# Attention probabilities transposed in 32x32 blocks on VectorE, with their partition groups exchanged by DMA through DRAM, in a hybrid encoder layer

## The reference, cut to what matters

```python
q_blocks = q_b.reshape(B, nb, Q_BLOCK, MLA_HEADS, hq).transpose(1, 0, 3, 2, 4)
scale = 1.0 / math.sqrt(hq)
def attend(qblk):
    s = jnp.einsum('bhqd,bhkd->bhqk', qblk, k_t).astype(jnp.float32) * scale
    p = jax.nn.softmax(s, axis=-1)
    return jnp.einsum('bhqk,bhkd->bhqd', p.astype(v_t.dtype), v_t)
```

## Time and profile before

| | |
|---|---|
| median of 3 runs | 1946.63 us |
| profiled execution | 1945.29 us, span from first to last instruction 1943.3 us |
| busy, share of the span | PE 97%, DVE 72%, ACT 54%, POOL 7% |
| MLA steps | first exponentials at 128.3 us, last at 523.3 us |
| first instruction of the GLA head (`gate_logits`) | 544.93 us |

### The profile page before, as it was taken

The page is one execution under the profiler, slowest core; times in us unless marked ns, Lnnn a source line. Parts: engine busy times, 40 slices in busy tenths (PEclk is TensorE's granted clock), DMA queues, the critical chain, the costliest instruction groups (busy, mean ns, idle before and its releaser), DMA issues.

```text
span 1943.3 us, 27074 instructions
## 1 busy us (share of the span) xinstructions
PE 1881.8 (97%) x9428; PEld 1598.5 (82%) x9428; DVE 1391.7 (72%) x1955; ACT 1049.3 (54%) x1726; POOL 135.8 (7%) x147
## 2 busy tenths in 40 slices
PE   9999999999999999999999999994799999999997
PEld 8988888888878888888888888884688888888886
DVE  4478777778865656657765348546799898998986
ACT  6476666555552434344434223321577777877775
POOL 1021101001000000000000000000000101001010
PEclk9999999999999999999999999997899999999999
DMA  6110000000321202022444463535899999999992
GB/s 208 44 43 7 23 23 18 23 25 18 125 62 32 66 23 77 11 76 87 139 156 150 140 205 109 184 130 197 318 379 400 391 401 399 392 400 390 400 391 77
DMA packets 147481, 327.57 MB, mean 169 GB/s; under 512 B 18080, under 2 KB 72736, under 8 KB 147232
## 3 DMA queue, kind: packets, MB, share of 16 engines
q1 hardware_dynamic: 142640, 309.59, 43.1%
q0 software_dynamic: 4752, 16.78, 3.4%
HBM read 287.92 MB, written 38.40 MB: 168 GB/s over the span
## 4 chain that ended last, share of the span: by engine, by line
PE 91%; DVE 5%; ACT 2%; DMA 1%; issue 1%; POOL 1%; SPq 0%; DVEq 0%; ACTq 0%; POOLq 0%
PE ps L1078 24%; PE ps L1080 24%; PE ps L1079 24%; PE ps L1067 7%; PE ps L1165 3%; PE ps L1373 1%; PE ps L1204 1%; PE ps L1203 1%; PE ps L1385 1%; PE ps L1357 1%; PE ps L1527 1%; PE ps L1383 1%; DVE top_i L2478 1%; DVE top_v L2477 1%; DMA xs<-in_x 1%
## 5 line engine op out<-in xcount | busy, mean ns | idle before, releaser
L1651 DVE TENSOR_TENSOR w_lo<-w_raw,w_hi 128x1024 fp32r<-128x1024 f32 x384 | 442.5, 1218 | 54.1 <-ACT w_hi L3054 53.9
L3054 ACT ACTIVATE w_hi<-w_raw 128x1024 fp32r<-128x1024 f32 x384 | 370.8, 1053 | 12.4 <-DMA w_raw<-in_w_gate_e 12.1
L1078 PE MATMUL ps<-w_hi,xeT_hi 128*128 128x512 f32 x512 | 201.0, 393 | 1.9 <-DVE xeT_lo L1651 1.0
L1080 PE MATMUL ps<-w_hi,xeT_lo 128*128 128x512 f32 x512 | 199.6, 390 | 0.0
L1079 PE MATMUL ps<-w_lo,xeT_hi 128*128 128x512 f32 x512 | 199.3, 389 | 0.0
L1651 DVE TENSOR_TENSOR d_lo<-d_raw,d_hi 128x1024 fp32r<-128x1024 f32 (+1 forms) x66 | 67.1, 1027 | 123.1 <-ACT d_hi L2716 118.5
L1078 PE MATMUL ps<-hT_parts,d_hi 128*128 128x512 f32 x368 | 144.7, 393 | 0.0
L1080 PE MATMUL ps<-hT_parts,d_lo 128*128 128x512 f32 x368 | 143.4, 390 | 0.0
L1079 PE MATMUL ps<-hT_parts,d_hi 128*128 128x512 f32 x368 | 143.3, 389 | 0.0
L985 POOL TENSOR_TENSOR stat<-stat,minus_half 128x4 f32<-128x4 f32 (+3 forms) x56 | 54.3, 971 | 1177.7 <-DVE stat L1648 1177.6
L1886 DVE TENSOR_REDUCE row_max<-ps 128x1 f32<-128x1024 f32 x64 | 78.3, 1224 | 79.1 <-PE ps L1204 79.1
(11 more groups left out here) (436 smaller groups left out, 4343.7 us busy)
## 6 DMA issues: line engine op xcount, KB each, us to landing
w_raw<-in_w_gate_e SPq DMA_DIRECT2D x128, 512.0 KB, 6.9
w_raw<-in_w_up_e SPq DMA_DIRECT2D x128, 512.0 KB, 6.9
w_raw<-in_w_down_e SPq DMA_DIRECT2D x128, 512.0 KB, 5.8
d_raw<-in_w_in SPq DMA_DIRECT2D x80, 256.0 KB, 3.3
gates_T<-stage SPq DMA_DIRECT2D x16, 512.0 KB, 2.6
sg<-gates_T SPq DMA_DIRECT2D x16, 512.0 KB, 3.6
stage<-mla_out_T SPq DMA_DIRECT2D x12, 512.0 KB, 5.3
xs<-in_x SPq DMA_DIRECT2D x8, 512.0 KB, 12.4
```

The source lines that it names most:

```text
L1078: pe.matmul(out_ap, a_hi, b_hi, start=start, stop=False)
L1080: return pe.matmul(out_ap, a_lo, b_hi, start=False, stop=stop)
L1651: return dve.tensor_tensor(dst, whole, high.bitcast(F32), ALU.subtract)
L3054: nc.scalar.activation(w_hi[:, n % RING, :], w_raw[:, n % RAW, :], ACT.Copy).then_inc(hi_ok, 1)
```

## The change

The transposition leaves PE. DVE transposes the normalised tile in 32x32 blocks (`squares_T`), within each group of 32 partitions. Blocks then still stand in the wrong group of partitions. SP writes each group of 32 partitions to DRAM (4 DMAs of 128 KB, `turn_probs`), waits for them, and reads the tile back as 128 rows of 4 KB, straight into `pT_lo`. ACT rounds it into `pT_hi` (one instruction from SBUF) and POOL subtracts in place to make `pT_lo`. `probs` has two buffers in place of three, `squares_T` has one. Columns of `pT_hi` and `pT_lo` are in another order, which a slice in `values` follows.

The order changes too: DVE normalises and transposes tile t at the end of step t, in place of normalising t-1 in the middle of it; the load of the hidden rows for the GLA stage is cut in 8 pieces of 512 KB, each waiting for the one before, among the turns of the last tiles; the second pair of `project_qk` comes before `values(7, 1)`.

```diff
+            def turn_probs(t):
+                sp.wait_ge(p_tr, t + 1)
+                if t:
+                    sp.wait_ge(p_in, 16 * t)
+                rows = p_dram[t % SLOTS].rearrange("(j b) q x -> b j q x", b=SQ)
+                for q in range(Q4):
+                    sp.dma_start(rows[:, :, q, :],
+                                 squares_T[q * SQ:(q + 1) * SQ].rearrange("b j c a -> b j (c a)")).then_inc(p_out, 16)
+                sp.wait_ge(p_out, 16 * Q4 * (t + 1))
+                group = t // Q4
+                if group >= 2:
+                    sp.wait_ge(pv_mm, group - 1)
+                sp.dma_start(probs_part(pT_lo, t).bitcast(F32),
+                             p_dram[t % SLOTS].rearrange("p q (c a) -> p q c a", a=SQ)).then_inc(p_in, 16)
...
-            for i in range(MH):
...
+            for i, n in STEPS:
+                if i < MH:
+                    turn_probs(8 * i + n)
...
+                if i >= MH - 1 and 2 <= 8 * i + n - 8 * (MH - 1) < 2 + KD:
+                    k = 8 * i + n - 8 * (MH - 1) - 2
...
+                    if k:
+                        sp.wait_ge(hT_in, 16 * k)
+                    sp.dma_start(hT_again[:, k, :], h_dram[k]).then_inc(hT_in, 16)
...
+            def probs_low(t):
+                pool.wait_ge(pt_hi, t + 1)
+                low = probs_part(pT_lo, t)
+                pool.tensor_tensor(low, low.bitcast(F32), probs_part(pT_hi, t).bitcast(F32),
+                                   ALU.subtract).then_inc(pt_lo, 1)
...
-            def probs_T(t):
-                pe.wait_ge(p_ok, t + 1)
-                for b in range(2):
...
-                    transpose4(4 + b, P, [probs[:, t % 3, (4 * b + j) * P:(4 * b + j + 1) * P]
-                                          for j in range(4)]).then_inc(p_tr, 1)
...
-                if tile_at(i, n) is not None:
-                    probs_T(tile_at(i, n))
+                if (i, n) == (MH, 2):
+                    for k in range(EARLY_ROWS, 4):
+                        project_qk(0, 0, k, first=True)
...
-                dve.tensor_scalar(probs[:, t % 3, :], probs[:, t % 3, :], row_inv[:, n:n + 1], None,
+                dve.tensor_scalar(probs[:, t % 2, :], probs[:, t % 2, :], row_inv[:, n:n + 1], None,
                                   ALU.mult).then_inc(p_ok, 1)
+                dve.wait_ge(p_ok, t + 1)
+                if t:
+                    dve.wait_ge(p_out, 16 * Q4 * t)
+                dve.transpose(squares_T[:], probs[:, t % 2, :].rearrange("p (c j b) -> p j c b", c=NT, j=Q4)) \
+                    .then_inc(p_tr, 1)
...
             def probs_high(t):
...
+                act.wait_ge(p_in, 16 * (t + 1))
+                nc.scalar.activation(probs_part(pT_hi, t), probs_part(pT_lo, t).bitcast(F32), ACT.Copy).then_inc(pt_hi, 1)
```

More of the change, by code:

```diff
@@ L993, in _, with keys_power, keys_rotary @@
                 rsqrt(stat[:, 1:3, t], mean_sq, mean_count(1, t), rstd)
-            for h in range(MH):
+            def keys_power(h):
                 rsqrt(stat[:, 5, :], mean_sq, HEAD_MEANS + 3 * h + 1, rstd)
+            def keys_rotary(h):
                 pool.wait_ge(rstd, HEAD_MEANS + 3 * h + 1)
@@ L1001, in _, with queries_power @@
                                    ALU.mult).then_inc(k_rot_ok, 1)
-                for half in range(2):
-                    rsqrt(stat[:, 4, 4 * half:4 * half + 4], mean_sq, HEAD_MEANS + 3 * h + half + 2, rstd)
+            def queries_power(h, half):
+                rsqrt(stat[:, 4, 4 * half:4 * half + 4], mean_sq, HEAD_MEANS + 3 * h + half + 2, rstd)
+            def probs_low(t):
[3 more added lines that the diff above has]
+                                   ALU.subtract).then_inc(pt_lo, 1)
+            keys_power(0)
+            keys_rotary(0)
+            queries_power(0, 0)
+            queries_power(0, 1)
+            for i, n in STEPS:
+                if n == 0 and i + 1 < MH:
+                    keys_power(i + 1)
+                if n == 2 and i + 1 < MH:
+                    queries_power(i + 1, 0)
+                if tile_at(i, n) is not None:
+                    probs_low(tile_at(i, n))
+                if n == 0 and i + 1 < MH:
+                    keys_rotary(i + 1)
+                if n == (3 if i else 4) and i + 1 < MH:
+                    queries_power(i + 1, 1)
             pool.wait_ge(pv_mm, 2 * MH)
@@ L1226, in values @@
                     mm = three(ps[:, 6, :], v_hi[h % 2][:, k, :], v_lo[h % 2][:, k, :],
-                               pT_hi[:, half, k, :], pT_lo[:, half, k, :], k == 0, k == NT - 1)
+                               pT_hi[:, half, :, k, :], pT_lo[:, half, :, k, :], k == 0, k == NT - 1)
                 if ks[-1] == NT - 1:
@@ L1457, in branch_job @@
                 mm.then_inc(d_used, 1)
-            for i in range(EARLY_ROWS, 4):
-                project_qk(0, 0, i, first=True)
             pe.wait_ge(ob_ev, 2 * MH)
@@ L2694, in probs_high @@
             def probs_high(t):
-                q = t % NT
-                for b in range(2):
-                    act.wait_ge(p_tr, 2 * t + b + 1)
-                    at = (slice(None), q // 4, slice(4 * b, 4 * b + 4), slice((q % 4) * P, (q % 4 + 1) * P))
-                    nc.scalar.activation(pT_hi[at], ps[:, 4 + b, :].rearrange("p (a c) -> p a c", a=4),
-                                         ACT.Copy).then_inc(pt_hi, 1)
+                act.wait_ge(p_in, 16 * (t + 1))
+                nc.scalar.activation(probs_part(pT_hi, t), probs_part(pT_lo, t).bitcast(F32), ACT.Copy).then_inc(pt_hi, 1)
             def exponentials(i, n):
```

89 lines of the change are left out of this document (40 added, 49 removed).

## The result

The changed kernel takes 2036.14 us (median of 4 runs, 2035.40 to 2036.91), the kernel before 1946.48 on the same chip: a ratio of 1.0459, 95% interval 1.0444 to 1.0475. It is slower, by 89.7 us. The profiled execution took 2036.91 us; its span is 2035.2, against 1943.3 before.

What follows compares the result with a forecast made beforehand. PE bounded the kernel before; SP's serial turn would replace it. First write 133.4, 64 turns of 7.0, tail 22.0 and heavy steps 4 put gate logits at 607.4 against 544.9: +62.5, so 2009 us, range 1965 to 2054.

Steps and rivals of the forecast that it cites:

- PE's saving: MLA stage: 512 transposes leave PE, 50.6 us, 6.71 to 5.92 us a tile, gained for nothing if SP sets the pace.
- The turn, L = 7.0: SP queue, each tile: writes 3.3, read 3.6 and gaps 0.1 us one after another, 7.0 us, 64 times.
- W: Time of a tile's four writes until all have landed: 3.3 us, between 3.15 and 3.7.
- heavy steps: Steps (i, 4), where DVE has extra work and runs over a turn: 2 to 8 us over 7 heads, taken as 4.
- signs of being wrong: Turn under 6.1 us, SP waiting for DVE in most tiles, or tail from last landing not near 22 us.
- In an ordinary step the tile is ready 2.4 us before SP wants it: From one landing to the tile after next, ACT and DVE take 4.6 us against 7.0 until the next landing.
- POOL's hold: POOL and DVE delaying each other: 0.9 us a tile, 55 us if on the path; 2.4 us spare in ordinary steps.
- POOL's low part, 1.90: POOL's subtraction for each tile: 1.90 us, far less than a turn, with only `values` waiting for it.
- DVE's transposition, X = 1.22: DVE's transposition of a tile in one pass, 1.22 us; rival of four passes, 4.9 us, giving 2107 us, chance 0.04.
- The tail: From the last tile's landing to the first gate logits: 22.0 us, with 5.5 for moving products ahead of `values`.
- PE stays the bound: Rival: turn under 6.09 us, so PE sets the pace and the kernel is faster, 1900 at best; chance 0.07.
- The narrow writes: Rival: writes from 32 partitions, or loads beside the reads, stretch the turn to 7.7 us, 2054 us; chance 0.20.

Runs made afterwards that it cites:

- the sliver: The pipelined queue kernel with POOL making the low part of only one column in 128: 1988.44 us, ratio 1.0220.
- Wide writes: The changed kernel with four writes of 128 partitions by 1 KB in place of 32 partitions by 4 KB: 2022.21 us, one run.
- the tail experiment: The changed kernel with the last two project_qk put back behind values(7, 1): 2026.99 us, ratio 1.0409.
- pipelined queue: The changed kernel with the wait for the read of tile t-1 moved behind tile t's writes, so both overlap: 2022.71 us, ratio 1.0386.
- the instruction beside: The sliver kernel with POOL also making the full low part after releasing PE, which reads high parts in both places: 2030.78 us, ratio 1.0437.

## Why the prediction came out as it did

The mechanism and the sign were right, and the time lay in the range, 27 us above the likeliest. By its own steps:

**PE's saving** counted for nothing, as said. PE is busy 89% of the stage, and that this is near the forecast 85% is luck: 5.92 us in turns of 7.43 would be 80%. PE was busy for 6.6 us a tile at a granted clock of 0.94, where 5.92 was read at 1.00; at 0.99, with the sliver, it was 5.95. From 133 to 600 us the clock averaged 0.90. The prediction looked at the clock only in the tail. PE's waits were forecast to be for the exponentials, or for POOL at `values`; from 200 to 500 us the profile puts 33 us of them down to DVE, nearly all to its low parts of q and k, and none to those two. (The 273 ns that the prediction calls a mean is the median of the earlier trace rows; nothing was computed from it.)

**The turn, L = 7.0.** Measured 7.43 in the mean, and SP's own waits show that it is the bound. This is the term that was mis-sized, and within it W alone: I took 3.3 from bounds of 3.15 and 3.7 and the trace has 3.69 in the median, 3.76 in the mean. The fourth write starts 1.3 us after the first, as forecast; the rest is the landing, 2.4 us where I had 1.85. In the median the first of the four lands after 2.04 us, the later ones after 2.36 to 2.41. I chose by the size of a write, "because the size is its size", and the row that mattered was the other one: the only store from fewer than 128 partitions. Wide writes landed in 1.9 and gave W = 3.3, so the choice missed by what the 32 partitions cost. The page "SBUF — State Buffer" of the Trainium skill (section "Door 1: The DMA port swizzle") pointed the right way; the estimate from its figure, W = 4.0, was 0.3 too high here. The read and its gap took 3.67 in the mean, forecast 3.7.

**The sum.** The first write went out at 133.86 (133.4 forecast). That is +0.5. Then 63 turns of 7.43 instead of 7.0 are +26.9, the last one +0.5, less the 4 us that I had put aside for heavy steps: the last tile landed at 609.28 (ACT's copy of it starts at 609.30) instead of 585.4. The tail is 634.38 - 609.28 = 25.1 instead of 22.0. Together 23.9 + 3.1 = 27.0, which is 634.38 - 607.4. Behind the gate logits everything was to move as a whole, but took 2.4 us longer (see the tail experiment). The median was to lie 1.3 us above the profiled execution and lies 0.8 below it, which hides that. In the prediction's range the upper end has the 4 us for heavy steps and the lower end has not: with them, L = 6.4 gives 1971 and not 1965. Of the signs of being wrong two did not show (no turn under 6.1, no waits for DVE in most tiles); the third did in part, a tail of 25.1 that was to be near 22.

**"In an ordinary step the tile is ready 2.4 us before SP wants it, and DVE's and ACT's changes cost nothing."** In the changed kernel this held narrowly: 4.8 us of waiting for DVE, but a margin of 1.4 us in the median and under 0.3 in a quarter of the tiles. As a statement on what stands behind the turn it was wrong. I added up one tile's chain with each instruction at its duration alone, and left out the rest of DVE's work, in order, and POOL. By the windows DVE was busy for 5.1 us a tile before and is busy for 6.3 now (253.06 us for 40.4 tiles), though it lost two low parts and gained a transposition. So wherever SP was made quicker, DVE took over at 7.2. The prediction named POOL's hold, priced it at 55 us if it lay on the path, and put it aside. In the changed kernel 30 of the 64 multiplications began while POOL was at its low part; they took 1.15 to 2.9 us and ended 0.55 us after POOL. The 33 without such an overlap took 0.75. The one of 1.61 us before had shown the same: it ended at 134.31, 0.54 after POOL's. Off SP's shadow it costs 34 us (pipelined queue, full low part against sliver), 42 with the instruction beside.

**POOL's low part, 1.90 from the row of the same shape.** It takes 2.39 in the median, 3.40 at most. The row had one operand that was repeated; this one reads two whole tiles and writes in place; which of these makes it longer was not tried. Only `values` waits for it, three times and 10.3 us in all; what that latency costs the changed kernel altogether was not measured.

**DVE's transposition, X = 1.22:** 1.245 in all 64, so one pass over 32-bit data. That rival is out.

**The heavy steps, 4 us:** about that, 4.8, but not where it was forecast. Steps (i, 4) have three of the ten waits, 0.7 us together; steps (i, 3), which got no term, have four and 1.8 us, and step (0, 7) alone has 1.6. The size is in part luck.

**The tail.** PE starts on rows 2 at 613.96, 4.7 after the landing (3.5 forecast): DVE's low parts of rows 2 and 3 take 3.67 us beside POOL's last low part, 2.47 before. Then 24 matmuls take 7.2 us and not 5.5, because most of the first ten come every 0.43 us at a granted clock of 0.58, near the lower of the two levels, 1.2 GHz: PE had waited 7.80 us before 607.53, and 1.82 again before 613.96. The rest is as forecast to 0.3 us. Putting the two products back gave 9.2 us where the prediction charged 5.5 for moving them; the clock has a share in that, in the matmuls above and in the 2.6 us behind the gate logits.

**The rivals.** "PE stays the bound" needed L under 6.09; no turn was under 6.88. The narrow writes were the right rival in kind, and half its size: W = 3.7, where 2054 needed 4.0. What stays open: no run had both the round trip and POOL gone (with POOL reduced to the sliver the round trip was overlapped, not removed), so what the tiles would cost at TensorE's pace is not shown, nor is POOL's share in the changed kernel as it stands, where it was not taken out alone. No version here beats the kernel before; the best that computes everything is the pipelined queue, 2022.7 us. The pipelined queue with the tail put back and nothing else was not run.

## What to carry to other kernels

A transposition moved off TensorE is paid in latency: write, wait, read, wait is a pace of its own, 7.4 us a tile here, to be held against the time a tile takes before, however idle the DMA engines are. The busy time that TensorE is spared need not show up as less busy time: once it waits, look at its granted clock. When such a serial pace is found, work out the next one behind it with every instruction of each engine in its order, and with what GpSimd does to VectorE at that moment, before saying what a quicker queue would give. And price a transfer by the row that is nearest in form (how many partitions), not only in size.

## What the runs showed of the hardware

- VectorE's multiplication of 128x1024 floats in SBUF (0.75 us) and its 128x128 steps (0.28 us) stood still until GpSimd's two-input instruction had ended: when that one had started first, the multiplication ended 0.55 us and the small steps 0.15 us after it, and they took up to 2.9 and 2.5 us in the changed kernel. The transposition (1.245 us in the median of every kernel), and the row maxima out of PSUM (means of 1.20 to 1.22), kept their duration beside the same instruction. The Trainium skill, page "SBUF — State Buffer", section "SBUF: two separate sides", states that VectorE and GpSimd hold their shared ports for a whole instruction, whichever starts first, and that of VectorE's instructions only those with two inputs in SBUF or in a mode that uses both ports ask for them. These numbers agree: the steps on q read two inputs, the transposition and the maxima one. The multiplication reads one tensor and was held, so by this rule it must have run in such a mode; no run here shows its mode. It also goes the other way: GpSimd's instruction, 2.39 us in the median, took up to 3.4, the longest beside a two-input step of VectorE (128x1024, 1.23 us) that had started first.
- Two neighbouring instructions of ScalarE swapped, with no work added, cost 14 us in two kernels, and the place of one multiplication and transposition in VectorE's order 66 to 69.
- A 128 KB write from 32 partitions landed after 2.4 us, the same bytes from 128 partitions after 1.9, one of 512 KB from 128 after 2.6 (medians).
- VectorE turned 32x32 blocks of 32-bit data at 1.245 us for 128x1024; a row maximum over the same shape takes 1.22.
- In the tail of the changed kernel the granted clock was 0.58 in a stretch in which TensorE was busy throughout, after waits of 7.8 and 1.8 us. From 133 to 523 us it averaged 0.92, with TensorE busy for 333 of the 390 us, against 1.00 with 387 of 390 before; the two levels are 1.2 and 2.4 GHz.
